# A two-layer fp32 model on one core: order of the k tiles and of the transposes where a norm begins without its root

## The chip, the cores and the metric

The kernel runs on one core of a Trainium2 chip. The metric is the device time in microseconds of one execution, as the median of several runs. TensorE (PE) multiplies matrices and writes PSUM banks; VectorE (DVE) and ScalarE (ACT) read PSUM and SBUF and do the element work; GpSimd (POOL) and SyncE (SP) mostly issue DMAs here.

## The reference, cut to what matters

A residual stream of 256 tokens by 1024 columns goes through two blocks. The first has two layers (a recurrent and attention mixer with a dense FFN, then gated linear attention with a mixture of 8 experts). The second has two layers, each an FFN, a hybrid mixer and another FFN. Everything is float32. At the head of every part stands the same step, a norm by rows with a gain by columns, and a product of its result with weights:

```
def rms_norm(x, g):
    xf = x.astype(jnp.float32)
    y = xf * lax.rsqrt(jnp.mean(xf * xf, axis=-1, keepdims=True) + EPS)
    return (y * g.astype(jnp.float32)).astype(x.dtype)

def swiglu(hn, w1, w3, w2):
    return (jax.nn.silu(hn @ w1) * (hn @ w3)) @ w2

h = h + even_mixer(rms_norm(h, norm_mix[0]), ...)
h = h + swiglu(rms_norm(h, norm_ffn[0]), ev_ffn_w1[j], ev_ffn_w3[j], ev_ffn_w2[j])
```

## The kernel before, in words

**Precision.** A float32 product is made of three fast products. Each operand is split in a rounded high part and the rest, so weights stand as `whi_ring` and `wlo_ring`, activations as `XHI` and `XLO`, and high by high, high by low and low by high are added in PSUM. ACT makes the high parts, by a copy that rounds; DVE makes the low parts, by subtraction.

**The residual** `H` has two token tiles (t = 0 and 1, 128 tokens each) of 1024 columns. The products want the columns on the partitions, so `H` is transposed in 8 k tiles of 128 columns (kt = 0 to 7). Two neighbouring k tiles share one PSUM bank: block b holds kt = 2b and 2b + 1, each with its 256 tokens, so four blocks hold them all. `turn_block` (line 974) transposes one block of one token tile.

**An entry** is what stands between the last product of one part and the first of the next. There are ten. In each, ACT's `gain` (line 1655) casts the eight k tiles from the banks to `XHI`, and DVE's `gain` (line 2322) writes the eight rests to `XLO`. PE then takes the k tiles one at a time in its first product. All three engines follow the list `X_ORDER`, which is (0, 2, 4, 6, 1, 3, 5, 7) before. On ACT an even k tile waits for its block's transposes (`tp_ready`). An odd one waits until DVE has done the even k tile of the same bank (`x_ready`), so that ACT and DVE do not read one bank at the same time. DVE's k tile waits for ACT's of the same number (`xhi_ready`), and PE's product for DVE's.

**The ten entries are of three kinds.**
- Six are without a root: the residual is transposed as it is, and the root of the mean square is applied after the product. They are the FFN of the first layer (near 119 us of the span), the mixer of the second (305), the router (424) and three FFNs of the second block (1754, 1942, 2271). PE runs `turn_sums` (line 980), ACT `ffn_entry` or `unrooted_entry`: the mean square of tile 0, the gain, the mean square of tile 1.
- Three have a root, which is multiplied in by the transposing product itself (`turn_norm`, and `turn_tiles` alone at the start): near 8, 1617 and 2135 us.
- One follows the experts (`turn_experts`, 1421 us). It begins with block pairs as soon as half of the last update is there.

**What releases what.** DVE writes the update of `H` in three instructions: token tile 0 (1024 columns, semaphore `h_ready`), the first 512 columns of token tile 1 (`half_ready`), and its last 512 (`h_ready` again). After a hybrid mixer or an FFN of the second block (`post`, line 2568 on) the update waits for a root of its own; in the first block (`residual`) it does not. `keep_busy` lets PE multiply constants, so that its clock isn't lowered while it has nothing to do.

**The order on each engine** is that of the program's text, each engine with its own stream and semaphores between them. No scheduler moves anything. Weights arrive by DMA in a ring of 6 chunks of 128 x 1024.

Of the kernel before, what the change touches and what calls it, by code (L numbers as in the profile page):

```python
# [41 lines left out]
MIX_ORDER = (2, 3, 0, 1, 6, 7, 4, 5)  # L42


X_ORDER = (0, 2, 4, 6, 1, 3, 5, 7)


def units(cols):
# [9 lines left out]
def build(nc, A, out):  # L58

    ctx = ExitStack()  # L60
    with ctx:
# [5 lines left out]
        def sem(name):  # L67
            return ctx.enter_context(nc.semaphore(name))
# [131 lines left out]
        s = {n: sem(n) for n in names}  # L200
# [50 lines left out]
        def col(name, i=0):  # L251
            if name == "norm_mix0":
                return FIRST_COLS[:, i:i + 1]
            tile, r = row_at[name]
            return COLS[:, tile, r + i:r + i + 1]
# [330 lines left out]
        def counter():  # L586
            n = {}

            def nxt(name, by=1):
                n[name] = n.get(name, 0) + by  # L590
                return n[name]
            return nxt
# [9 lines left out]
        def _(pe):  # L602
            nxt = counter()
# [12 lines left out]
            def unit(ph, u, lo=0, hi=KT, banks=None, bank_unused=False):  # L616
# [5 lines left out]
                for i, _, k0, kn in pieces:  # L622
                    c_ = ph["c0"] + i
                    wh, wl = (w[:, c_ % RING, 0:kn * n].rearrange("p (k n) -> p k n", k=kn) for w in (WHI, WLO))
                    for kt in X_ORDER if u == 0 else range(KT):
                        if not max(k0, lo) <= kt < min(k0 + kn, hi):
# [17 lines left out]
            def up(c_, slot, q, qb, first, n):  # L644

                wait(pe, "bank_free", q - 1)
                for half in range(2):
# [16 lines left out]
                    if first and half == 0:  # L664
                        for kt in X_ORDER:
                            pe.wait_ge(s["xhi_ready"], nxt("xhi_ready"))
# [32 lines left out]
            def keep_busy(bank, n):  # L699
                for _ in range(n):  # L700
                    mm(BANK[bank][:, 0:P], IDENT[:, :], IDENT[:, :], start=True, stop=True)
# [272 lines left out]
            def turn_block(banks, t, b):  # L974
                for kt in (2 * b, 2 * b + 1):
                    last = tr(BANK[banks[b]][:, (2 * (kt % 2) + t) * P:(2 * (kt % 2) + t + 1) * P],
                              H[:, t, kt * P:(kt + 1) * P], IDENT[:, :])
                return last

            def turn_sums(banks, busy=0):  # L980

                nxt("ssq_ready", 2)
                h = nxt("h_ready", 2)
                spare = 4 - banks[3]
                keep_busy(spare, busy // 3)
                pe.wait_ge(s["h_ready"], h - 1)
                for b in range(4):
                    turn_block(banks, 0, b)
                keep_busy(spare, busy)
                pe.wait_ge(s["half_ready"], nxt("half_ready"))  # L990
                for b in range(4):
                    if b == 2:
                        pe.wait_ge(s["h_ready"], h)
                    turn_block(banks, 1, b).then_inc(s["tp_ready"], 1)

            def turn_experts():

# [251 lines left out]
            def router():  # L1249
                for kt in X_ORDER:  # L1250
                    pe.wait_ge(s["x_ready"], nxt("x_ready"))
                    for a, (w, x) in enumerate(((0, XHI), (1, XHI), (0, XLO))):
                        last = mm(BANK[2][0:NE, 0:S], RTP[w][:, kt, :], x[:, kt, :],
                                  start=(kt == 0 and a == 0), stop=(kt == KT - 1 and a == 2))
                last.then_inc(s["score_ready"], 1)
                pe.wait_ge(s["logit_ready"], 17)
                for t in range(TT):
                    last = tr(BANK[3][:, t * NE:(t + 1) * NE], LOGT[:, t * P:(t + 1) * P], IDENT[0:NE, 0:NE])
                last.then_inc(s["score_ready"], 1)
                keep_busy(7, 12)  # L1260

                pe.wait_ge(s["msk_ready"], 1)
                mm(BANK[1][:, 16:24], ONES[:, :], MSK[:, 0, :], start=True, stop=False)
                mm(BANK[1][:, 16:24], ONES[:, :], MSK[:, 1, :], start=False, stop=True).then_inc(s["pos_mm"], 1)
                mm(BANK[0][:, 0:8], UPPER[:, :], MSK[:, 0, :], start=True, stop=True)
                mm(BANK[0][:, 8:16], ONES[:, :], MSK[:, 0, :], start=True, stop=False)
                mm(BANK[0][:, 8:16], UPPER[:, :], MSK[:, 1, :], start=False, stop=True).then_inc(s["pos_mm"], 1)
# [305 lines left out]
            turn_tiles()  # L1573
            even_mixer(EV_PROJ, EV_OUT)
            turn_sums(turned(EV_FFN))
            ffn(EV_FFN)
            turn_sums(TURNED_MID)
            nxt("xhi_ready", KT)
            odd_mixer(OD_PROJ, OD_OUT)
            nxt("xhi_ready", KT)  # L1580
            turn_sums(TURNED_LOW)
            nxt("xhi_ready", KT)
            router()
# [22 lines left out]
        def _(act):  # L1606
            nxt = counter()
# [25 lines left out]
            def unrooted_entry(name, banks):  # L1633
                act.wait_ge(s["h_ready"], nxt("h_ready"))
                mean_square(0, HN[:, 0, :])
                act.wait_ge(s["h_ready"], nxt("h_ready"))
                gain(name, banks)
                mean_square(1, HN[:, 0, :])

            def ffn_entry(name, banks=TURNED):  # L1640
                act.wait_ge(s["h_ready"], nxt("h_ready"))
                mean_square(0, HN[:, 0, :])
                act.wait_ge(s["h_ready"], nxt("h_ready"))
                gain(name, banks)
                mean_square(1, HN[:, 0, :])
                af(SCRATCH_COL, EPS_COL, ACT.Silu)

            def mean_square(t, squares=None):

                af(HN[:, t, :] if squares is None else squares, H[:, t, :], ACT.Square, scale=D ** -0.5, accum_out=STAT[:, t:t + 1])\  # L1650
                    .then_inc(s["ssq_ready"], 1)
                act.wait_ge(s["ssq_ready"], nxt("ssq_ready"))
                af(STAT[:, 34 + t:35 + t], STAT[:, t:t + 1], ACT.Sqrt, bias=EPS_COL).then_inc(s["root_of_ssq"], 1)

            def gain(name, banks=TURNED):

                x_at = nxt("x_ready", KT) - KT
                for i, kt in enumerate(X_ORDER):
                    b, j = kt // 2, kt % 2
                    if j:  # L1660
                        act.wait_ge(s["x_ready"], x_at + X_ORDER.index(kt - 1) + 1)
                    else:
                        act.wait_ge(s["tp_ready"], nxt("tp_ready"))
                    af(XHI[:, kt, :], BANK[banks[b]][:, j * S:(j + 1) * S], ACT.Copy, scale=col(name, kt))\
                        .then_inc(s["xhi_ready"], 1)
# [532 lines left out]
            gain("norm_mix0")  # L2198
            even_mixer(EV_PROJ, EV_OUT)
            ffn_entry("norm_ffn0", turned(EV_FFN))  # L2200
            ffn(EV_FFN)
            unrooted_entry("norm_mix1", TURNED_MID)
            odd_mixer(OD_PROJ, OD_OUT)
            unrooted_entry("norm_ffn1", TURNED_LOW)
            crowded = router()
            with act.If(crowded):
# [7 lines left out]
            for l in range(2):  # L2214
                f1, pr, ou, f2 = HY[l]
                if l:
                    ffn_entry(f"ffn1_pre{l}", turned(f1))
                else:
                    ahead(f1["c0"])
                    norm()  # L2220
                    af(SCRATCH_COL, EPS_COL, ACT.Silu)
                ffn(f1, begun=(l == 0))
                post(f1)
                norm()
                gain(f"mix_pre{l}")
                hybrid(l, pr, ou)
                post(ou)
                ffn_entry(f"ffn2_pre{l}", turned(f2))
                ffn(f2)
                post(f2)  # L2230
# [3 lines left out]
        def _(dve):  # L2234
# [87 lines left out]
            def gain(name, banks=TURNED):  # L2322
                for kt in X_ORDER:
                    b, j = kt // 2, kt % 2
                    dve.wait_ge(s["xhi_ready"], nxt("xhi_ready"))
                    V_.scalar_tensor_tensor(XLO[:, kt, :], BANK[banks[b]][:, j * S:(j + 1) * S], col(name, kt),  # L2326
                                            XHI[:, kt, :].bitcast(F32), ALU.mult, ALU.subtract)\
                        .then_inc(s["x_ready"], 1)
# [1011 lines left out]
```

## Time and profile before

| | |
|---|---|
| median of 3 runs | 2469.18 us (2467.38 to 2470.3) |
| the profiled execution's own time | 2467.24 us |
| its span (first to last instruction) | 2465.5 us |
| PE busy | 2437.7 us, 99% of the span |
| DVE busy | 2034.6 us, 83% |
| ACT busy | 1544.8 us, 63% |
| mean granted TensorE clock | 0.998 |

PE is busy nearly all the time, and the chain that ends last runs mostly over it. What PE does in an entry is therefore the question: there it waits for work of DVE and ACT, and part of its busy time is transposes or constants. A row with "x8" holds eight instructions; the time beside the start runs from the start of the first to the end of the last, and instructions of one engine may overlap.

### The profile page before, as it was taken

Reading aid. Unit: us, or ns where it says so; the run is one execution under the profiler, and the core shown is the slowest. Engines: PE = TensorE matmul, PEld = TensorE weight load, DVE = VectorE, ACT = ScalarE, POOL = GpSimd, SP = SyncE. Lnnn points to the kernel's source line nnn. Section 1 sums busy time; section 2 is a strip of 40 time slices with the busy share of each in tenths; the row PEclk is TensorE's granted clock in tenths of the full one; section 3 lists DMA queues with packets and bytes.
Section 4 is the critical chain, followed back from the end, with each engine's and each line's share of the span. In section 5 each row is a group of like instructions: output and inputs, shape, how many; then the busy total and the mean of one; then the engine's idle time right before and its main releaser. Section 6 shows DMA issues by size and latency. Waiting matters only on the chain.

```text
span 2465.5 us, 39205 instructions
## 1 busy us (share of the span) xinstructions
PE 2437.7 (99%) x14162; PEld 2083.5 (85%) x14162; DVE 2034.6 (83%) x2978; ACT 1544.8 (63%) x2153; POOL 73.2 (3%) x158
## 2 busy tenths in 40 slices
PE   9999999999999999999999999999999999999998
PEld 8888887788888888888888888899888888898887
DVE  7777766889898989998999987789877877798776
ACT  6754555677777777777777764463644644644544
POOL 9000000000000000000000000000000000000000
PEclk9999999999999999999999999999999999999999
DMA  7466643699999999999999966643566566533663
GB/s 213 147 189 187 179 154 128 232 370 367 354 359 375 366 351 359 377 362 352 368 373 365 365 201 195 187 122 103 173 187 195 174 194 187 154 101 115 197 195 111
DMA packets 481949, 596.82 MB, mean 242 GB/s; under 512 B 21922, under 2 KB 313202, under 8 KB 481808
## 3 DMA queue, kind: packets, MB, share of 16 engines
q1 hardware_dynamic: 478208, 589.47, 71.4%
q0 software_dynamic: 3600, 5.48, 0.8%
q8 instruction: 86, 1.41, 0.2%
q14 instruction: 55, 0.45, 0.1%
HBM read 593.83 MB, written 1.05 MB: 241 GB/s over the span
## 4 chain that ended last, share of the span: by engine, by line
PE 91%; DVE 5%; ACT 2%; issue 1%; DMA 0%; SPq 0%; DVEq 0%; ACTq 0%
PE bank L893 25%; PE bank L654 16%; PE bank L919 12%; PE bank L688 10%; PE bank L660 8%; PE bank L639 5%; PE bank L636 2%; PE bank L1524 1%; DVE wlo_ring L2248 1%; PE bank L904 1%; PE bank L1241 1%; PE bank L1069 1%; PE bank L736 1%; PE bank L760 1%; DVE h L2598 1%
## 5 line engine op out<-in xcount | busy, mean ns | idle before, releaser
L2248 DVE TENSOR_TENSOR wlo_ring<-raw_ring,whi_ring 128x1024 fp32r<-128x1024 f32 (+1 forms) x1122 | 1331.3, 1219 | 116.0 <-ACT whi_ring L1616 96.0
L1616 ACT CAST whi_ring<-raw_ring 128x1024 fp32r<-128x1024 f32 (+1 forms) x1122 | 1145.5, 1051 | 165.2 <-DMA raw_ring<-in_od_exp_w_dram 153.3
L654 PE MATMUL bank<-x,whi_ring 128*128 128x512 f32 x1720 | 427.3, 391 | 0.0
L654 PEld LDWEIGHTS bank<-x,whi_ring 128*128 128x128 f32 x1720 | 315.6, 188 | 60.9
L660 PEld LDWEIGHTS bank<-x,wlo_ring 128*128 128x128 f32 x1720 | 220.9, 191 | 9.4 <-DVE wlo_ring L2248 1.0
L660 PE MATMUL bank<-x,wlo_ring 128*128 128x256 f32 x1720 | 223.8, 283 | 0.8 <-DVE wlo_ring L2248 0.8
L1690 ACT COPY arena<-bank 128x256 f32<-128x256 f32 x110 | 40.9, 372 | 268.8 <-PE bank L660 268.8
L639 PE MATMUL bank<-x,whi_ring 128*128 128x256 f32 (+2 forms) x1024 | 193.0, 289 | 0.7 <-DVE x L2326 0.6
L893 PE MATMUL bank<-whi_ring,xg0hi 128*128 128x512 f32 x448 | 178.3, 398 | 2.9 <-DVE xg0lo L2397 2.9
L893 PE MATMUL bank<-whi_ring,xg1hi 128*128 128x512 f32 x448 | 177.2, 395 | 0.0
L893 PE MATMUL bank<-whi_ring,xg0lo 128*128 128x512 f32 x448 | 175.5, 392 | 0.0
L893 PE MATMUL bank<-wlo_ring,xg0hi 128*128 128x512 f32 x448 | 175.5, 392 | 0.0
L893 PE MATMUL bank<-whi_ring,xg1lo 128*128 128x512 f32 x448 | 174.8, 390 | 0.0
L893 PE MATMUL bank<-wlo_ring,xg1hi 128*128 128x512 f32 x448 | 174.6, 390 | 0.0
L639 PEld LDWEIGHTS bank<-x,whi_ring 128*128 128x128 f32 (+2 forms) x1024 | 155.7, 188 | 8.1 <-issue 2.9
L2344 DVE TENSOR_TENSOR arena<-arena,bank 128x256 f32<-128x256 f32 x110 | 46.2, 420 | 134.4 <-ACT arena L1690 134.3
L639 PE MATMUL bank<-x,wlo_ring 128*128 128x256 f32 (+1 forms) x512 | 144.5, 282 | 0.0
L919 PE MATMUL bank<-whi_ring,hidhi 128*128 128x512 f32 x440 | 135.6, 389 | 0.0
L919 PE MATMUL bank<-wlo_ring,hidhi 128*128 128x512 f32 x440 | 135.5, 389 | 0.0
L919 PE MATMUL bank<-whi_ring,hidlo 128*128 128x512 f32 x440 | 135.5, 389 | 0.0
L1696 ACT COPY arena<-bank 128x256 f32<-128x256 f32 x110 | 41.0, 372 | 149.5 <-PE bank L654 149.5
L688 PE MATMUL bank<-whi_ring,hidhi 128*128 128x512 f32 x380 | 117.1, 389 | 1.7 <-DVE hidlo L2363 1.7
(540 smaller groups left out, 3576.0 us busy)
## 6 DMA issues: line engine op xcount, KB each, us to landing
raw_ring<-in_od_exp_w_dram SPq DMA_DIRECT2D x672, 512.0 KB, 5.5
raw_ring<-in_ffn_w_gate_dram SPq DMA_DIRECT2D x88, 512.0 KB, 3.9
raw_ring<-in_ffn_w_up_dram SPq DMA_DIRECT2D x88, 512.0 KB, 5.0
raw_ring<-in_ffn_w_down_dram SPq DMA_DIRECT2D x88, 512.0 KB, 3.5
raw_ring<-in_ev_ffn_w_dram SPq DMA_DIRECT2D x66, 512.0 KB, 4.0
raw_ring<-in_w_in_dram SPq DMA_DIRECT2D x42, 512.0 KB, 4.1
raw_ring<-in_od_w_in_dram SPq DMA_DIRECT2D x24, 512.0 KB, 4.3
raw_ring<-in_ev_w_in_dram SPq DMA_DIRECT2D x20, 512.0 KB, 7.0
```

The costliest lines, as they stand in the source:

```text
L636: last = mm(banks[t] if banks else row_bank(q, n, t), x[:, kt, t * P:(t + 1) * P], w[:, kk, :], start=st and (n > 256 or t == 0), stop=sp_ ...
L639: last = mm(BANK[q % 2][0:n, 0:S], w[:, kk, :], x[:, kt, :], start=st, stop=sp_)
L654: mm_ = mm(bank[:, :], wh[:, kt, :], X2[:, kt, :, :].rearrange("p a n -> p (a n)"), start=(start and kt == 0), stop=(stop and kt == KT - 1 ...
L660: mm_ = mm(bank[:, 0:S], wl[:, kt, :], XHI[:, kt, :], start=(start and kt == 0), stop=(stop and kt == KT - 1), skip_group_check=True)
L688: last = mm(pair[h][:, :], x[:, b, t * P:(t + 1) * P], w[:, h * 512:(h + 1) * 512], start=(start and a == 0), stop=False, skip_group_check ...
L893: last = mm(bank[:, :], x[:, kt, slots], w[:, kk, :], start=(kt == 0 and a == 0), stop=(kt == KT - 1 and a == 2))
L919: last = mm(BANK[4 + h][:, :], x[:, j * P:(j + 1) * P], w[:, h * 512:(h + 1) * 512], start=(g == 0 and j == 0 and a == 0), stop=(g == GROU ...
L1616: nc.scalar.copy(WHI[:, slot, 0:n], RAW[:, slot, 0:n]).then_inc(s["hi_ready"], 1)
L1690: nc.scalar.copy(GATE_LO[:, b, :], BANK[2 * b][:, S:2 * S]).then_inc(s["gate_lo"], 1)
L1696: nc.scalar.copy(UP_LO[:, b, :], BANK[2 * b + 1][:, S:2 * S]).then_inc(s["up_lo"], 1)
L2248: V_.tensor_tensor(WLO[:, slot, 0:n], RAW[:, slot, 0:n], WHI[:, slot, 0:n].bitcast(F32), ALU.subtract)\
L2344: V_.tensor_tensor(GATE[:, qb, :], GATE_LO[:, qb, :], BANK[2 * qb][:, 0:S], ALU.add)\
```

## The change

Three edits, with the same instructions as before in another order.

1. `X_ORDER` becomes (0, 2, 1, 3, 4, 6, 5, 7), for all ten entries and on all three engines: both k tiles of blocks 0 and 1 come first, then those of blocks 2 and 3.
2. In `turn_sums`, PE transposes blocks 0 and 1 of token tile 0, waits for `half_ready`, transposes blocks 0 and 1 of token tile 1, then blocks 2 and 3 of token tile 0, waits for `h_ready`, and then does blocks 2 and 3 of token tile 1. Before, all of token tile 0 came first.
3. In `unrooted_entry` and `ffn_entry`, ACT's wait for the second `h_ready` (all of token tile 1) moves from ahead of the gain to behind it. The gain then waits for its blocks only.

```
-X_ORDER = (0, 2, 4, 6, 1, 3, 5, 7)
+X_ORDER = (0, 2, 1, 3, 4, 6, 5, 7)
...
                 pe.wait_ge(s["h_ready"], h - 1)
-                for b in range(4):
-                    turn_block(banks, 0, b)
-                keep_busy(spare, busy)
-                pe.wait_ge(s["half_ready"], nxt("half_ready"))
-                for b in range(4):
-                    if b == 2:
+                for pair in ((0, 1), (2, 3)):
+                    for b in pair:
+                        turn_block(banks, 0, b)
+                    if pair[0] == 0:
+                        keep_busy(spare, busy)
+                        pe.wait_ge(s["half_ready"], nxt("half_ready"))
+                    else:
                         pe.wait_ge(s["h_ready"], h)
-                    turn_block(banks, 1, b).then_inc(s["tp_ready"], 1)
+                    for b in pair:
+                        turn_block(banks, 1, b).then_inc(s["tp_ready"], 1)
...
             def unrooted_entry(name, banks):
                 act.wait_ge(s["h_ready"], nxt("h_ready"))
                 mean_square(0, HN[:, 0, :])
+                gain(name, banks)
                 act.wait_ge(s["h_ready"], nxt("h_ready"))
-                gain(name, banks)
                 mean_square(1, HN[:, 0, :])
```

`ffn_entry` has the same exchange of two lines.

The next rows are ACT's, in the entry of the first FFN, before. In their names `arena,stat<-h` is the mean square of a token tile, and `x2<-bank,cols` is a cast of the gain.

```order
L1650 ACTIVATE arena,stat<-h 128x1024 [waits h_ready]
L1653 ACTIVATE stat<-stat 128x1 [waits ssq_ready]
L1664 ACTIVATE x2<-bank,cols 128x256 [waits tp_ready,h_ready]
L1664 ACTIVATE x2<-bank,cols 128x256 [waits tp_ready] x3
L1664 ACTIVATE x2<-bank,cols 128x256 [waits x_ready] x4
L1650 ACTIVATE arena,stat<-h 128x1024
```

The same place on ACT now:

```order
L1652 ACTIVATE arena,stat<-h 128x1024 [waits h_ready]
L1655 ACTIVATE stat<-stat 128x1 [waits ssq_ready]
L1666 ACTIVATE x2<-bank,cols 128x256 [waits tp_ready] x2
L1666 ACTIVATE x2<-bank,cols 128x256 [waits x_ready] x2
L1666 ACTIVATE x2<-bank,cols 128x256 [waits tp_ready] x2
L1666 ACTIVATE x2<-bank,cols 128x256 [waits x_ready] x2
L1652 ACTIVATE arena,stat<-h 128x1024 [waits h_ready]
```

The wait for `h_ready` has moved from the first cast to the second mean square, and the casts that wait for DVE stand in third and fourth, seventh and eighth place.

The next rows are PE's in the same entry, before; `bank<-ident,h` is a transpose of one k tile of one token tile.

```order
L976 MATMUL bank<-ident,h 128x128 [waits h_ready]
L976 MATMUL bank<-ident,h 128x128 x7
L976 MATMUL bank<-ident,h 128x128 [waits half_ready]
L976 MATMUL bank<-ident,h 128x128 x3
L976 MATMUL bank<-ident,h 128x128 [waits h_ready]
```

And PE's now:

```order
L976 MATMUL bank<-ident,h 128x128 [waits h_ready]
L976 MATMUL bank<-ident,h 128x128 x3
L976 MATMUL bank<-ident,h 128x128 [waits half_ready]
L976 MATMUL bank<-ident,h 128x128 x7
L976 MATMUL bank<-ident,h 128x128 [waits h_ready]
```

The wait for `half_ready` has moved ahead by four transposes, and after the wait for `h_ready` four are left, as before.

## Rows read from the trace of the kernel before

**Rows 1.** The page's part 4, the chain that ended last, by engine.

```profile
PE 91%; DVE 5%; ACT 2%; issue 1%; DMA 0%; SPq 0%; DVEq 0%; ACTq 0%
```

**Rows 2.** ACT's casts, line 1664: what ended ACT's idle time before them (us, times).

```profile
PE bank L960: 5.3, 3
DVE h L2598: 3.8, 3
PE bank L976: 3.1, 3
```

**Rows 3.** DVE's rests and PE's transposes: durations in ns (least, median, most).

```profile
L2326 DVE SCALAR_TENSOR_TENSOR x<-bank,cols,x x72: 472/476/488, 121.1 to 2277.9; 128x256 fp32r<-128x256 f32 x72
...
L976 PE MATMUL bank<-ident,h x112: 271/273/329, 119.1 to 2275.1; 128*128 128x128 f32 x112
```

**Rows 4.** Timeline, entry of the first FFN: start, length in us, engine, line, tiles.

```profile
117.86 2.42 DVE L2550 TENSOR_TENSOR h<-h,bank 128x1024 f32<-128x1024 f32 x3 [4.42 <-PE bank L1069]
...
120.31 0.29 ACT L1653 ACTIVATE stat<-stat 128x1 f32<-128x1 f32 x1
120.63 3.03 ACT L1664 ACTIVATE x<-bank,cols 128x256 fp32r<-128x256 f32 x8
121.14 3.22 DVE L2326 SCALAR_TENSOR_TENSOR x<-bank,cols,x 128x256 fp32r<-128x256 f32 x8 [0.86 <-ACT x L1664]
```

**Rows 5.** The chain that ended last, same entry: start, length, what.

```profile
117.86 1.23 DVE h L2550
119.09 0.02 issue
```

**Rows 6.** Timeline, entry of the second layer's mixer.

```profile
304.88 1.91 PE L976 MATMUL bank<-ident,h 128*128 128x128 f32 x16
305.08 0.75 DVE L2548 SCALAR_TENSOR_TENSOR h<-bank,stat,h 128x512 f32<-128x512 f32 x1 [1.33 <-PE bank L736]
306.23 3.03 ACT L1664 ACTIVATE x<-bank,cols 128x256 fp32r<-128x256 f32 x8 [2.37 <-PE bank L976]
306.74 3.23 DVE L2326 SCALAR_TENSOR_TENSOR x<-bank,cols,x 128x256 fp32r<-128x256 f32 x8 [0.91 <-ACT x L1664]
```

**Rows 7.** Timeline, the router's entry.

```profile
425.22 3.09 ACT L1664 ACTIVATE x<-bank,cols 128x256 fp32r<-128x256 f32 x8
...
426.15 3.22 DVE L2326 SCALAR_TENSOR_TENSOR x<-bank,cols,x 128x256 fp32r<-128x256 f32 x8
```

**Rows 8.** Timeline, entry of an FFN behind a hybrid mixer (the three alike).

```profile
1753.51 1.09 PE L976 MATMUL bank<-ident,h 128*128 128x128 f32 x8 [1.03 <-DVE h L2598]
...
1755.58 1.42 DVE L2598 SCALAR_TENSOR_TENSOR h<-arena,stat,h 128x512 f32<-128x512 f32 x2
1756.45 1.26 PE L976 MATMUL bank<-ident,h 128*128 128x128 f32 x8
...
1757.03 3.03 ACT L1664 ACTIVATE x<-bank,cols 128x256 fp32r<-128x256 f32 x8 [1.25 <-DVE h L2598]
1757.54 3.23 DVE L2326 SCALAR_TENSOR_TENSOR x<-bank,cols,x 128x256 fp32r<-128x256 f32 x8 [0.55 <-ACT x L1664]
```

**Rows 9.** Timeline, entry of a hybrid mixer, with its root.

```profile
1619.89 3.28 ACT L1664 ACTIVATE x<-bank,cols 128x256 fp32r<-128x256 f32 x8 [2.22 <-PE bank L960]
1620.39 3.39 DVE L2326 SCALAR_TENSOR_TENSOR x<-bank,cols,x 128x256 fp32r<-128x256 f32 x8 [1.58 <-ACT x L1664]
```

**Rows 10.** Timeline, the entry behind the experts.

```profile
1422.51 0.92 DVE L2326 SCALAR_TENSOR_TENSOR x<-bank,cols,x 128x256 fp32r<-128x256 f32 x2
...
1423.83 2.49 DVE L2326 SCALAR_TENSOR_TENSOR x<-bank,cols,x 128x256 fp32r<-128x256 f32 x6 [0.39 <-ACT x L1664]
```

**Rows 11.** Windows of 2 us behind the router: busy time by engine, granted clock.

```profile
436.00:438.00 2.00, 2.00 (x16) 2.00 (x17) 1.93 (x6) 0.86 (x2) 0.00 (x0) 0.83 0.00 0
438.00:440.00 2.00, 2.00 (x11) 2.00 (x11) 2.00 (x3) 0.00 (x0) 0.00 (x0) 0.50 0.00 0
440.00:442.00 2.00, 2.00 (x16) 2.00 (x16) 0.73 (x1) 0.00 (x0) 0.00 (x0) 0.82 0.56 131
```

More of the change, by code:

```diff
@@ L1642, in ffn_entry @@
                 mean_square(0, HN[:, 0, :])
+                gain(name, banks)
                 act.wait_ge(s["h_ready"], nxt("h_ready"))
-                gain(name, banks)
                 mean_square(1, HN[:, 0, :])
```

## The prediction

> **What bounds the kernel now.** I began with the chain that ended last: 91% of it is PE, 5% DVE, 2% ACT [rows 1]. So an instruction moved on ACT or DVE counts only where PE waits for it, and PE waits for both in the ten entries. Next I asked what ACT's casts wait for. Before them ACT idled 5.3 us in three entries for transposes with a root, 3.8 us in three for the last update of `H`, 3.1 us in three for transposes without a root [rows 2]. Edit 3 can touch only the 3.8 us, edit 2 a part of the 3.1 us. Last I read the timeline of one entry of each kind [rows 4, 6 to 10]. In all of them the eight rests on DVE stand close together and PE's products keep their pace: the last rest is what sets the end of an entry. So I work out, for every entry, when DVE's eighth rest starts, before and after.
>
> **The durations.** From ACT's first cast to DVE's first rest is 120.63 to 121.14, or 0.51 us [rows 4]; it is 0.51 again in the second layer's mixer and behind a hybrid mixer [rows 6, 8]. A rest lasts 0.476 us [rows 3], but eight of them take 3.22, so they start (3.22 - 0.476)/7 = 0.392 us apart [rows 4]. ACT's casts, each also about 0.48 long, start (3.03 - 0.48)/7 = 0.365 apart. A semaphore takes 0.02 to 0.03 us from one engine to the other: token tile 0 of `H` is ready at 119.09 and ACT starts 0.02 later [rows 5]. I take 0.03.
>
> **Edit 1, the list.** An odd k tile's cast waits for DVE's rest of the even one in its bank. Before, the two stood four places apart, and the rest was long done. Now they are two apart. Call the start of DVE's first rest 0. It ends at 0.476, ACT starts the third cast at 0.51, and DVE the third rest 0.51 later, at 1.02. At its own pace DVE would have started it at 2 x 0.392 = 0.784, so DVE stands still for 0.235 us. The fourth cast waits for the second rest (0.392 + 0.51 = 0.90) and the fourth rest starts at 1.41, which is 0.392 behind the third: no further loss. The fifth and sixth casts wait for transposes only, and ACT regains its lead (fifth cast at 1.27, rest at 1.80). The seventh waits for the fifth rest, and 0.235 us is lost a second time. The eighth rest starts at 3.21 instead of 2.74: **0.47 us later in an entry whose start doesn't move.** Two ends for the price: nothing, if a cast went ahead of the wait; and two full ACT-to-DVE steps, 1.02 us, if nothing overlapped. I take 0.47, since each step of it is in the rows of this very pair of instructions.
>
> The page "VectorE: DVE Perf Modes" of the Trainium skill, section "The DRAIN you can't avoid", says that the next VectorE op does not start until the pipe is empty. If that held, rests would start 0.476 apart, the third at 0.95 anyway, and the loop would lose 0.07 instead of 0.235, 0.14 an entry. The trace disagrees: 0.392 us apart for a duration of 0.476 [rows 3, 4].
>
> The page "PSUM — Partial Sum Buffer" of the Trainium skill, section "PSUM bank collisions raise a hardware error", lets ScalarE and VectorE read at the same time only in different banks, and asks for a semaphore by bank. That is the wait which the new list makes late; no run here shows what its absence would do.
>
> **Edits 2 and 3, by kind of entry.**
>
> First FFN: ACT ends the mean square of tile 0 at 120.31 + 0.29 = 120.60, and the update of `H` was finished at 117.86 + 2.42 = 120.28 [rows 4]. The wait that is moved was already met. The first cast stays at 120.63: +0.47. PE's new order of transposes is hidden behind the mean square too.
>
> Router: ACT begins to cast at 425.22 and DVE only at 426.15, since it has a root to make first [rows 7]. The start is DVE's and doesn't move; the loop binds from there: +0.47.
>
> Second layer's mixer: PE starts the transposes at 304.88, long after the first half of the update, and the first block is complete behind ten of them, the cast at 306.23 [rows 6]. Now it is complete behind six. Sixteen take 1.91 us and the last one 0.27 [rows 3], so they stand (1.91 - 0.27)/15 = 0.109 apart, and four are 0.44 us. DVE's update ends at 305.83, early enough: -0.44 + 0.47 = +0.03.
>
> Three FFNs of the second block: ACT casts at 1757.03, released by the end of the update. The first half of it ends at 1755.58 + 0.75 = 1756.33, as long as the same shape in rows 6. PE is then free: four transposes have gone from ahead of its constants, which end at 1755.98 instead of 1756.45 [rows 8]. Two transposes (0.11 apart, 0.27 long [rows 3]) complete block 0 at 1756.74, the cast starts at 1756.77 and the rest at 1757.28, behind the update's end at 1757.00. That is 0.26 sooner than 1757.54: -0.26 + 0.47 = +0.21, three times +0.63. Blocks 2 and 3 come some 1.2 us before ACT needs them.
>
> Three entries with a root: only edit 1 touches them. The second cast waits for block 1, (3.28 - 0.48 - 4 x 0.365)/3 = 0.45 us behind the first, and the eighth rest starts 3.39 - 0.476 = 2.91 behind the first [rows 9]. The same reckoning gives rests at 0, 0.45, 1.02, 1.48, 1.87, 2.26, 2.89 and 3.28: +0.37, three times +1.11. The old list lost part of this to transposes already.
>
> Entry behind the experts: rests at 1422.51 and 1422.95, then a wait for the second half, and the last at 1423.83 + 2.49 - 0.48 = 1425.84 [rows 10]. Now two more k tiles (1 and 3) are at hand before that half: rests at 1423.53 and 1423.97, and the last at 1425.77: -0.07.
>
> **The sum** is 0.47 + 0.47 + 0.03 + 0.63 + 1.11 - 0.07 = +2.6 us. The profiled execution took 2467.24 us, 1.7 us more than its span; it would become 2469.9. The median of the runs is 1.9 us above that execution, so I forecast 2469.2 + 2.6 = 2471.8 us. All of it is pieces of half a microsecond, 0.1% in the whole. Behind an entry little can give it back: ACT and DVE begin their weight casts later by the same step, since they stood in the entry too. ACT ends its gain later by more, 0.67 us in the first FFN (its eighth cast starts at 121.14 + 2.70 instead of 120.63 + 2.55). I take the 0.2 us that are over as hidden, for PE first works through weight chunks that are already split; uncovered in all ten entries they would be 2 us, which the range holds.
>
> **The rivals.**
>
> *The loop costs nothing.* DVE hides the wait, as by the rule on the drain above. For it: the margin is 0.235 us, a few hundred nanoseconds. Against: each link is measured. Only the earlier starts count: -0.44 - 3 x 0.26 - 0.07 = -1.3 us, 2467.9.
>
> *Hidden anyway.* PE leaves an entry later and catches up, because what it waits for next (a weight's low part, a root) was the later one all the time. For it: DVE casts weights without rest. Against: 91% of the chain is PE. Both shifts and gains are lost in part: +0.5 us, 2469.7.
>
> *The early start doesn't come.* The casts still begin where they began, because block 0 arrives late. Then edits 2 and 3 give nothing, and only the loops are left: 6 x 0.47 + 1.11 - 0.07 = +3.9 us, 2473.1. Against: the half update and PE's free time are both in rows 8.
>
> *Slower, by the clock.* PE now stands still twice more in each entry, and in the FFN entries of the second block also 0.4 us before the half update, since its four transposes no longer fill that gap. Behind the router the granted clock fell to the lower level, 1.2 of 2.4 GHz, for about 3.4 us: 2 x (0.17 + 0.50 + 0.18) = 1.7 us lost [rows 11]. Should three more entries lose as much, 5.1 + 2.6 = +7.7 us, 2476.9. It decides from two such falls on (2.6 + 3.4 = 6.0). Against: the mean clock of the whole span was 0.998, which leaves 0.002 x 2465.5 = 4.9 us for all falls together, so the ten entries had next to none, with a gap of 1.03 us before the transposes of an FFN among them [rows 8].
>
> The page "TensorE: Matmul & The Clock Gate" of the Trainium skill, section "Terms", puts the penalty at the throttled time times the share of pulses held back: 3.4 x 0.5 = 1.7 us, as the rows give.
>
> **Chances.** Forecast 62%, no loop 13%, hidden 12%, no early start 4%, clock 9%. What a measurement of this kernel can tell from no change is about 0.2%, 4.9 us. Only the clock rival passes it clearly, and the forecast with its scatter seldom: slower 10%, the same 87%, faster 3%. The range, 2467 to 2476, takes in the loop at nothing (2467.9), the loop at its upper end in part, one fall of the clock (2473.5), and the scatter of the medians (1.5 us to either side).
>
> **What would show it.** In each entry the third and the seventh rest on DVE start 1.02 us behind the first and the fifth, and the eight rests take 3.7 instead of 3.22 us. ACT's casts show waits for DVE in place of the 3.8 us for the update; these are gone. The first cast moves by 0.44 in the second layer's mixer, by 0.26 in three FFNs, and not at all in the first FFN and the router. I am wrong if the eight rests still take 3.2 us, if PE's span behind the entries doesn't move with them, or if the clock shows a fall that wasn't there.

## The result, and the profile after

The changed kernel takes 2470.93 us (median of 20 runs, 2468.89 to 2473.71) against 2468.43 (20 runs, 2464.22 to 2470.3) for the kernel before. The ratio is 1.0013, with a 95% interval of 1.0007 to 1.0019. That is 1.7 to 4.7 us more, and below the 0.2% at which I would speak of a change, though the interval leaves out a ratio of 1. The forecast was 2.6 us more, at 2471.8.

The shape of every entry has changed in the way the trace was asked to show. This is the timeline of the first FFN's entry after the change (start, length in us, engine, line, tiles); ACT's casts are line 1666 now and DVE's rests line 2328. It answers to [rows 4].

```profile
118.06 2.42 DVE L2552 TENSOR_TENSOR h<-h,bank 128x1024 f32<-128x1024 f32 x3 [4.43 <-PE bank L1071]
...
120.50 0.30 ACT L1655 ACTIVATE stat<-stat 128x1 f32<-128x1 f32 x1
120.83 0.84 ACT L1666 ACTIVATE x<-bank,cols 128x256 fp32r<-128x256 f32 x2
121.33 0.88 DVE L2328 SCALAR_TENSOR_TENSOR x<-bank,cols,x 128x256 fp32r<-128x256 f32 x2 [0.85 <-ACT x L1666]
121.85 1.60 ACT L1666 ACTIVATE x<-bank,cols 128x256 fp32r<-128x256 f32 x4 [0.19 <-DVE x L2328]
...
122.36 1.66 DVE L2328 SCALAR_TENSOR_TENSOR x<-bank,cols,x 128x256 fp32r<-128x256 f32 x4 [0.15 <-ACT x L1666]
...
123.67 0.87 ACT L1666 ACTIVATE x<-bank,cols 128x256 fp32r<-128x256 f32 x2 [0.22 <-DVE x L2328]
124.17 0.88 DVE L2328 SCALAR_TENSOR_TENSOR x<-bank,cols,x 128x256 fp32r<-128x256 f32 x2 [0.15 <-ACT x L1666]
```

Read it from the breaks. One row of eight casts has become rows of 2, 4 and 2, and so has the row of eight rests. Each break on ACT ends with "<-DVE x", each on DVE with "<-ACT x": the two engines wait for one another in turn. The third rest starts 1.03 us behind the first (forecast: 1.02). The eight take 121.33 to 125.05, or 3.72 us, where they took 3.22. The first cast has not moved against the update of `H` ahead of it (2.77 us behind its start, before and after).

What ended ACT's idle time before the casts, after the change; it answers to [rows 2] (us, times):

```profile
PE bank L976: 5.5, 5
PE bank L960: 5.2, 3
DVE x L2328: 3.9, 17
```

The waits for the update are gone, as edit 3 says, and two new things stand in their place: ACT waits for transposes in those entries, and 17 times for DVE. On PE, the weight loads of the FFNs' first products show the same loss. This is what ended PE's idle time before line 670; before, it was 1.1 us in 4 times.

```profile
DVE x L2328: 3.2, 10
```

The entry of the second layer's mixer, which answers to [rows 6]:

```profile
305.56 1.91 PE L976 MATMUL bank<-ident,h 128*128 128x128 f32 x16
305.76 0.75 DVE L2550 SCALAR_TENSOR_TENSOR h<-bank,stat,h 128x512 f32<-128x512 f32 x1 [1.33 <-PE bank L736]
306.42 0.84 ACT L1666 ACTIVATE x<-bank,cols 128x256 fp32r<-128x256 f32 x2 [1.87 <-PE bank L976]
```

The first cast comes 0.86 us behind the start of the transposes, not 1.35. That is 0.49 sooner, and the loop takes it all back: the last rest ends 4.87 us behind the start of the last update, before it was 4.89.

The entry of an FFN behind a hybrid mixer, which answers to [rows 8]:

```profile
1758.36 0.66 PE L976 MATMUL bank<-ident,h 128*128 128x128 f32 x4 [1.03 <-DVE h L2600]
1758.85 2.17 PE L701 MATMUL bank<-ident 128*128 128x128 f32 x18
...
1760.43 1.41 DVE L2600 SCALAR_TENSOR_TENSOR h<-arena,stat,h 128x512 f32<-128x512 f32 x2
1761.24 1.53 PE L976 MATMUL bank<-ident,h 128*128 128x128 f32 x12 [0.21 <-DVE h L2600]
...
1761.71 0.84 ACT L1666 ACTIVATE x<-bank,cols 128x256 fp32r<-128x256 f32 x2 [1.08 <-PE bank L976]
```

The cast comes 1.28 us behind the start of the first half update, before 1.45. It gained 0.17, where I had said 0.26. The transposes did move ahead of the constants' old end, but PE now waits for the half update ("0.21 <-DVE h") and starts 0.81 behind its start, not 0.78; from there the cast is 0.47 away, where I had reckoned 0.41.

All ten entries, by the length of the eight rests and by the shift of the last rest's end against what leads into the entry (the update of `H` or the transposes), from the two profiles:

| entry | rests before | rests after | shift | forecast |
|---|---|---|---|---|
| first FFN | 3.22 | 3.72 | +0.49 | +0.47 |
| router | 3.22 | 3.71 | +0.49 | +0.47 |
| second layer's mixer | 3.23 | 3.70 | -0.02 | +0.03 |
| three FFNs | 3.23, 3.22, 3.23 | 3.72, 3.73, 3.72 | +0.32 to +0.33 | +0.21 |
| three with a root | 3.33, 3.39, 3.39 | 3.71, 3.77, 3.78 | +0.38 to +0.39 | +0.37 |
| behind the experts | 3.81 | 3.76 | -0.05 | -0.07 |

The sum is 3.0 us. The two profiled executions differ by 6.2 us (spans 2465.5 and 2471.7), so about 3.2 lie elsewhere. They lie between the router and the entry behind the experts: from the router's last rest to the first rest there it is 993.1 us before and 996.5 after. Whether that is the change was open, and the experiments had to say.

The clock: windows behind the router, after, which answer to [rows 11].

```profile
436.00:438.00 2.00, 1.37 (x10) 1.29 (x10) 1.93 (x6) 1.97 (x3) 0.00 (x0) 0.88 0.00 0
438.00:440.00 2.00, 2.00 (x12) 2.00 (x11) 2.00 (x4) 0.01 (x1) 0.00 (x0) 0.50 0.00 0
440.00:442.00 2.00, 2.00 (x15) 2.00 (x15) 1.87 (x2) 0.00 (x0) 0.00 (x0) 0.77 0.12 16
```

This fall is the same: 2 x (0.12 + 0.50 + 0.23) = 1.7 us lost, as before. There is a second one some 10 us later, in both profiles. These are windows of the kernel before and of the changed one:

```profile
448.00:450.00 2.00, 2.00 (x6) 1.52 (x6) 1.33 (x2) 1.15 (x2) 0.00 (x0) 0.50 0.54 136
...
448.00:450.00 2.00, 2.00 (x6) 1.52 (x6) 0.94 (x2) 0.00 (x0) 0.00 (x0) 0.50 0.13 19
```

With its neighbours it costs 1.7 us again, before (0.89, 0.50 and 0.76 in three windows) and after (0.94, 0.50 and 0.71). So the two profiles compared here have the same two falls, and the ten entries, where the granted clock is 1.00 in both, have none.

### The profile page after: what moved, and what is told of

Same layout as the page of the kernel before. It is cut to its first block, busy times and chain, and to the rows that moved or that the text cites. A ratio compares the mean times of both kernels' runs of the same rounds, so it can differ in the third digit from the quotient of the medians.

```text
span 2471.7 us, 39199 instructions
## 1 busy us (share of the span) xinstructions
PE 2441.8 (99%) x14162; PEld 2083.6 (84%) x14162; DVE 2035.7 (82%) x2978; ACT 1545.8 (63%) x2153; POOL 72.8 (3%) x158
## 4 chain that ended last, share of the span: by engine, by line
PE 85%; DVE 8%; ACT 3%; DMA 3%; issue 2%; SPq 0%; DVEq 0%; ACTq 0%
PE bank L893 22%; PE bank L654 16%; PE bank L688 10%; PE bank L919 10%; PE bank L660 8%; PE bank L639 5%; DVE wlo_ring L2250 3%; PE bank L636 2%; DMA raw_ring<-in_od_exp_w_dram 2%; PE bank L1526 1%; ACT whi_ring L1618 1%; PE bank L904 1%; PE bank L1243 1%; PE bank L1071 1%; PE bank L736 1%
```

## The experiments

The theory was that the guard on a bank makes ACT and DVE wait for one another when an odd k tile stands two places behind the even one, 0.235 us twice an entry. Its rivals were that DVE's pace hides it, and that the time is lost elsewhere, in the experts. The first four ran in one series with 27 runs of the kernel before (median 2467.87 us).

**The new list alone.** Against the kernel before:

```
-X_ORDER = (0, 2, 4, 6, 1, 3, 5, 7)
+X_ORDER = (0, 2, 1, 3, 4, 6, 5, 7)
```

> Only edit 1, the list (0, 2, 1, 3, 4, 6, 5, 7); transposes and ACT's waits as before. Theory (the loop through the bank's guard costs 0.235 us twice an entry): the eight rests on DVE take 3.7 us in the six entries without a root and 3.8 with one, the starts don't move, and the sum is 6 x 0.47 + 3 x 0.37 - 0.07 = +3.9 us over the kernel before. Rival 1 (the loop is hidden by DVE's own pace): the eight rests take 3.2 us, and the time is within 0.3 us of before. Rival 2 (what is lost stands in the stretch of the experts, not in the entries): the rests take 3.7, but the time grows by more than 5 us, the surplus between the router and the entry behind the experts.

Measured: 2471.53 us, ratio 1.0017 (1.0007 to 1.0026), which is 3.7 us more in the medians; 3.9 was forecast. The eight rests take 3.71 or 3.72 us in the entries without a root, 3.77 in the two of the hybrid mixers. The stretch of the experts is 993.15 us here, as in the kernel before. So the loss is in the entries, and both rivals fall.

**Edits 2 and 3 alone**, with the old list. Against the changed kernel:

```
-X_ORDER = (0, 2, 1, 3, 4, 6, 5, 7)
+X_ORDER = (0, 2, 4, 6, 1, 3, 5, 7)
```

> Edits 2 and 3 without edit 1: the list stays (0, 2, 4, 6, 1, 3, 5, 7). Theory: no loop, the eight rests take 3.2 us everywhere; the first cast comes 0.44 us sooner in the second layer's mixer, 0.2 to 0.3 sooner in three FFNs of the second block, and the whole is 1.0 to 1.2 us faster than before, 3.9 faster than all three edits. Rival (the early start needs the new list, because the third cast, of k tile 4, waits for the last update): the first cast comes sooner, the third doesn't, and only the 0.44 is left.

Measured: 2467.49 us, ratio 0.9997 (0.9988 to 1.0006). The interval holds both the 1.0 to 1.2 us of the theory and nothing at all. The profile tells more. This is the entry of an FFN:

```profile
1757.84 1.41 DVE L2600 SCALAR_TENSOR_TENSOR h<-arena,stat,h 128x512 f32<-128x512 f32 x2
...
1759.12 3.17 ACT L1666 ACTIVATE x<-bank,cols 128x256 fp32r<-128x256 f32 x8 [1.08 <-PE bank L976]
1759.63 3.32 DVE L2328 SCALAR_TENSOR_TENSOR x<-bank,cols,x 128x256 fp32r<-128x256 f32 x8 [0.37 <-ACT x L1666]
```

The first cast is 0.17 sooner, but the rests take 3.32 us. The third cast waits for block 2 with the old list, near to what the rival said, though only 0.1 us of it shows; that it is tile 0's part of the block, which edit 2 has put behind the half update, and not the update's last half, is what the run of edit 3 alone says below. The last rest ends 5.11 us behind the start of the half update, before 5.19: 0.08 gained in each of three FFNs. In the second layer's mixer it ends 4.48 behind the last update's start, before 4.89: 0.41. That makes 0.65 us in all. The theory was right on the loop and put the gain too high: 1.0 to 1.2 us was forecast.

**All three edits, odd tiles at least three places behind.** Against the changed kernel:

```
-X_ORDER = (0, 2, 1, 3, 4, 6, 5, 7)
+X_ORDER = (0, 2, 4, 1, 6, 3, 5, 7)
```

> All three edits, but the list is (0, 2, 4, 1, 6, 3, 5, 7): every odd k tile stands at least three places behind the even one of its bank. Theory: three places are enough (a rest ends at 0.476 + 0.03, the fourth cast would start at 0.585 anyway), so there is no stall of DVE in any entry, eight rests in 3.2 us, and with the early starts the whole is 1.2 to 1.5 us faster than before and about 4 faster than the three edits. Rival (it is the mixing of odd and even tiles as such that costs, by two engines reading PSUM more closely together): rests or casts last longer than 0.48 us, and eight of them take over 3.4.

Measured: 2467.02 us, ratio 0.9997 (0.9988 to 1.0006). Its median lies 3.9 below the changed kernel's, over two series, and 0.9 below the kernel before, where 1.2 to 1.5 were forecast. The interval doesn't tell 0.9 from nothing, but the profile does: measured as in the table above, the ten last rests come 0.9 us sooner in all. The second layer's mixer and an FFN:

```profile
305.63 2.81 ACT L1666 ACTIVATE x<-bank,cols 128x256 fp32r<-128x256 f32 x7 [1.87 <-PE bank L976]
...
1756.57 3.17 ACT L1666 ACTIVATE x<-bank,cols 128x256 fp32r<-128x256 f32 x8 [1.08 <-PE bank L976]
1757.08 3.32 DVE L2328 SCALAR_TENSOR_TENSOR x<-bank,cols,x 128x256 fp32r<-128x256 f32 x8 [0.37 <-ACT x L1666]
```

No break at the odd tiles: one place more between a k tile and its neighbour in the bank is enough. The rests take 3.23 in the first FFN, 3.22 at the router, and 3.33 or 3.34 in the hybrid mixers' entries, a little less than the 3.39 of before. So mixing odd and even tiles costs nothing; the distance does. In the mixer and the three FFNs the rests take 3.32 and not the 3.2 that were forecast, for the same reason as with the old list: the third cast (k tile 4) waits for block 2. This is the fastest of the orders in the medians.

**The guard met at every odd tile**, against the kernel before:

```
-X_ORDER = (0, 2, 4, 6, 1, 3, 5, 7)
+X_ORDER = (0, 1, 2, 3, 4, 5, 6, 7)
```

> The kernel before with the list (0, 1, 2, 3, 4, 5, 6, 7): an odd k tile stands right behind the even one of its bank, so the loop is met four times an entry with nothing between. Theory: a pair of rests takes 1.02 + 0.39 us, the eighth rest starts 4 x 1.02 + 3 x 0.39 = 5.26 us behind the first instead of 2.74. That is +2.5 us in six entries, +2.35 in three with a root, +1.9 behind the experts, +24 us in all (ratio 1.010). Rival (the loop is hidden or cheap): under +5 us.

Measured: 2491.72 us, ratio 1.0097 (1.0081 to 1.0112), 23.9 us more in the medians; 24 was forecast. A pair, in an FFN's entry:

```profile
1771.77 0.48 DVE L2326 SCALAR_TENSOR_TENSOR x<-bank,cols,x 128x256 fp32r<-128x256 f32 x1 [0.54 <-ACT x L1664]
1772.29 0.84 ACT L1664 ACTIVATE x<-bank,cols 128x256 fp32r<-128x256 f32 x2 [0.55 <-DVE x L2326]
...
1772.80 0.88 DVE L2326 SCALAR_TENSOR_TENSOR x<-bank,cols,x 128x256 fp32r<-128x256 f32 x2 [0.54 <-ACT x L1664]
...
1777.05 0.48 DVE L2326 SCALAR_TENSOR_TENSOR x<-bank,cols,x 128x256 fp32r<-128x256 f32 x1 [0.54 <-ACT x L1664]
```

The round from rest to cast to rest is 1772.80 - 1771.77 = 1.03 us, and the eighth rest starts 5.28 us behind the first (5.26 was reckoned). This is the experiment that settles the theory: its cost is six times the half width of its interval.

**Edit 2 alone.** Against the kernel before, in `turn_sums`:

```
-                for b in range(4):
-                    turn_block(banks, 0, b)
...
+                for pair in ((0, 1), (2, 3)):
+                    for b in pair:
+                        turn_block(banks, 0, b)
...
+                    for b in pair:
+                        turn_block(banks, 1, b).then_inc(s["tp_ready"], 1)
```

> Edit 2 alone (PE's order of transposes), old list, ACT's wait ahead of the gain. Theory: the first cast of the second layer's mixer waits for the update's end now (0.03 behind it) instead of for ten transposes, and so comes some 0.4 us sooner, measured from the start of the transposes; in the three FFNs of the second block the cast stays where it was, right behind the update, since ACT's wait holds it. Rival: no cast moves, because both edits are needed.

One execution (2464.73 us; the stretch of the experts was short in it, 991.2). The second layer's mixer and an FFN:

```profile
304.73 1.91 PE L976 MATMUL bank<-ident,h 128*128 128x128 f32 x16
...
305.71 2.68 ACT L1666 ACTIVATE x<-bank,cols 128x256 fp32r<-128x256 f32 x7 [2.00 <-DVE h L2550]
...
1753.14 1.42 DVE L2600 SCALAR_TENSOR_TENSOR h<-arena,stat,h 128x512 f32<-128x512 f32 x2
...
1754.59 3.03 ACT L1666 ACTIVATE x<-bank,cols 128x256 fp32r<-128x256 f32 x8 [1.26 <-DVE h L2600]
```

The mixer's cast is 0.98 behind the start of the transposes instead of 1.35, and it is the update that releases it now. In the FFN it stays 1.45 behind the half update. The last rest of the mixer ends 4.52 us behind the last update's start, before 4.89: 0.37 gained. As the theory said; the rival falls.

**Edit 3 alone.** Against the kernel before, in both entry functions:

```
                 mean_square(0, HN[:, 0, :])
+                gain(name, banks)
                 act.wait_ge(s["h_ready"], nxt("h_ready"))
-                gain(name, banks)
                 mean_square(1, HN[:, 0, :])
```

> Edit 3 alone (ACT's wait for all of token tile 1 behind the gain), old list, old order of transposes. Theory: the cast of the second layer's mixer stays behind ten transposes; in three FFNs of the second block block 0 is complete two transposes after PE's constants end, 0.87 us after the start of the first half update plus 0.4, so that the cast comes 0.15 us sooner than before, less than the 0.17 to 0.18 us that both edits gave (the after profile). Rival: it comes no sooner, or as early as with both.

One execution (2466.66 us). The same entry of an FFN:

```profile
1755.52 1.42 DVE L2598 SCALAR_TENSOR_TENSOR h<-arena,stat,h 128x512 f32<-128x512 f32 x2
1756.38 1.27 PE L976 MATMUL bank<-ident,h 128*128 128x128 f32 x8
1756.80 3.03 ACT L1664 ACTIVATE x<-bank,cols 128x256 fp32r<-128x256 f32 x8 [1.09 <-PE bank L976]
```

The cast comes 1.28 behind the half update, as early as with both edits. That is the rival of this run, and not the theory, which had the cast a little later. Edit 2 buys nothing in these FFNs. Without it PE turns from its constants to the transposes without a pause, 0.86 behind the half update, and the cast follows 0.42 later; with it PE stands still, starts at 0.81 and the cast follows 0.47 later. The rests take 3.23 us here and not 3.32, for tile 0 is transposed in full before the half update, and block 2 needs nothing more than its second half. The last rest ends 5.02 behind the half update, before 5.19: 0.17 gained, against 0.08 with both edits. The mixer's first cast is 1.29 behind the transposes' start, 0.06 sooner than before. The update whose wait was moved had ended 0.40 us ahead of the cast in the kernel before, at 305.83 against 306.23, so the wait was long met; why it still cost 0.06 isn't shown. In all, edit 3 alone gains about 0.6 us, edit 2 alone about 0.4, both together 0.65.

**Both kernels once more**, for their profiles.

> The kernel before once more, for one more profile. Open is the stretch from the end of the router's entry to the entry behind the experts: 993.1 us in the profile of before, 996.5 in that of after, 993.2 with the new list alone, 995.9 without it. Theory (it scatters by some 3 us from execution to execution, whatever the kernel): another value between 993 and 997 here, not the 993.1 again. Rival (edits 2 and 3 lengthen it): 993.1 to 993.4 again.

> The changed kernel once more, for the same question. Theory (scatter): the stretch from the router to the experts' end takes another value between 993 and 997. Rival (the change lengthens it): 996 or more again. The ten entries take the same as in the first profile of it, to 0.05 us.

Measured: 2467.77 us before, 2469.36 after, one time each. The stretch of the experts is 993.4 us in this profile of before (993.1 in the first) and 992.4 in this one of after (996.5 in the first). Over the ten profiles of all kernels it lies between 991.2 and 996.5, and 995.9 is met with the old list. The changed kernel alone spans 4.1 us, and its second value is below both of before. So the 3.4 us of the first comparison are not the change's. Two forecasts were missed here: the kernel before took 993.4, which was the rival's value, and the changed one 992.4, below the 993 to 997 of the theory.

What makes the stretch long or short stands in part in the profiles. Two things differ from one to the other, whatever the kernel: how often the granted clock fell between 434 and 464 us, and the share of the weights' DMA in the chain of waits over the stretch.

| profile | falls | DMA in the chain | stretch, us |
|---|---|---|---|
| edit 2 alone | 1 | 0.7% | 991.2 |
| changed, second | 1 | 2.0% | 992.4 |
| every odd tile guarded | 1 | 0.8% | 992.8 |
| before, second | 1 | 3.7% | 993.4 |
| before, first | 2 | 0.0% | 993.1 |
| the new list alone | 2 | 0.0% | 993.2 |
| all three, spaced | 2 | 0.0% | 993.4 |
| edit 3 alone | 2 | 1.4% | 993.4 |
| edits 2 and 3 | 2 | 5.9% | 995.9 |
| changed, first | 2 | 5.6% | 996.5 |

The second profile of the kernel before has one fall and the first has two. In a window where the first shows a clock of 0.83 it shows 1.00 (first and second profile):

```profile
434.00:444.00 10.00, 9.14 (x62) 8.85 (x62) 6.91 (x13) 4.47 (x9) 0.00 (x0) 0.83 0.31 101
...
434.00:444.00 10.00, 7.59 (x62) 7.31 (x62) 8.44 (x20) 6.04 (x12) 0.00 (x0) 1.00 0.29 90
```

A fall costs 1.7 us. So the two profiles of the kernel before agree to 0.3 us although they differ in both: the second has a fall less and waits more for DMA. The two longest stretches have two falls and the most DMA in the chain. Why the clock falls once or twice, and why the DMA is late in some executions, was not tested. These are the chain's rows for the changed kernel, first and second profile (each goes on with smaller shares):

```profile
by line: PE bank L893 53.4%; PE bank L919 25.2%; DMA raw_ring<-in_od_exp_w_dram 5.6%; DVE wlo_ring L2250 4.2%; PE bank L904 2.2%; PE bank L760 1.4%; ACT whi_ring L1618 1.2%; issue 1.2%; PE bank L847 0.7%; PE bank L848 0.6%; PE bank L934 0.6
```

```profile
by line: PE bank L893 58.5%; PE bank L919 27.9%; DVE wlo_ring L2250 2.4%; PE bank L904 2.3%; DMA raw_ring<-in_od_exp_w_dram 2.0%; PE bank L760 1.4%; PE bank L847 0.7%; PE bank L848 0.6%; issue 0.6%; PE bank L934 0.6%; ACT whi_ring L1618 0.5
```

The entries are the same in both profiles of after, to 0.02 us.

## Why the prediction was right

**The loop.** Right in mechanism and size: 0.49 us an entry for the 0.47 reckoned, 0.38 to 0.39 for 0.37 with a root, and the amplified form of it (+24 us) came within 0.2 us. The rule that the prediction cites from the page "VectorE: DVE Perf Modes" of the Trainium skill, section "The DRAIN you can't avoid", would have made it 0.14 and is not borne out here: rests of 0.48 us start 0.39 to 0.40 apart in every profile. The same section goes on to say that a next op that is not held starts earlier. The prediction left that out, so the rows speak against the rule as it was quoted and not against the section.

**No start in the first FFN and the router.** Right: the casts stand where they stood, behind the mean square and behind the root that DVE makes.

**The mixer of the second layer.** Right: -0.02 for +0.03. The two edits gain 0.49 (0.44 was reckoned for four transposes less) and the loop takes it.

**Three FFNs.** The one term mis-sized: the earlier start was put at 0.26 and is 0.17, so each costs 0.32 to 0.33 and not 0.21. I had let PE start the transposes 0.03 behind the half update and taken the delay of a running stream from there. From a standstill PE starts 0.06 behind it and the cast comes 0.06 later than reckoned, 0.47 behind that start and not 0.41. The term as a whole was +0.63 and is about +1.0. The prediction also has blocks 2 and 3 ready some 1.2 us before ACT needs them; by its own numbers block 2 is complete about 0.9 us before its cast, which changes nothing in the sum.

**Behind the experts.** Right: -0.05 for -0.07.

**Nothing given back.** Right: from the last rest in the first FFN to the transposes of the next mixer it is 180.5 us in both profiles. The same holds behind the other entries: from the last rest of one to what leads into the next, the nine lengths outside the experts' stretch (the last one up to the end) agree within 0.15 us over all ten profiles.

**The rivals.** No loop: refuted by the list alone and by the pairs. Hidden anyway: refuted by the same 180.5 us. No early start: refuted in two kinds of entry. The clock: it fell no more often than before. The prediction counted one fall behind the router, 1.7 us; the profiles before and after have two there, 3.4 us together. That leaves the rival refuted.

**The sum** was +2.6, the entries give +3.0, the medians +2.5 and the interval 1.7 to 4.7. That the medians meet the forecast to 0.1 us is luck: the term of the three FFNs alone is 0.3 us short, and the whole times cannot tell 2.5 from 3.0.

## What to carry to other kernels

Two engines that take turns on one resource under a guard have a round-trip time; an order of work is free of it only if the guarded neighbours stand far enough apart. Here the round is 1.03 us against steps of 0.39, so two places cost and three don't. Bringing work forward pays only where it is waited for: edits 2 and 3 together are worth about 0.65 us with the old list, while the new list, whose earlier odd tiles nobody waited for, costs 3.7 alone.

For an edit of half a microsecond, the lengths within a profile repeat to 0.02 us while whole executions scatter by 5: compare the stretch, and enlarge the suspected cost until the whole time shows it.

## What the runs showed of the hardware that I had not expected

A PE that waits at the semaphore is slower off the mark than one that is working. Behind the wait its first two transposes start 0.16 to 0.17 us apart and the next ones 0.11; in a running stream the first two are 0.11 apart as well. So the transposes start 0.81 us behind the half update and the cast follows 0.47 later with the pause, 0.86 and 0.42 without, and freeing PE 0.5 us sooner gave nothing.

The experts' stretch, the same instructions each time, took from 991.2 to 996.5 us over ten profiles: more than the change under test. The granted clock fell once or twice in it, at 1.7 us a fall, and the two longest are those in which the chain waited most for DMA.
